# The joints between six sites of a two-part transformer kernel, worked tile by tile

## The reference

```python
def second_block(x, ...):
    for layer in range(2):
        g = norm_gains[layer]
        x = x + 0.5 * rmsnorm(swiglu(rmsnorm(x, g[0]), ...[layer, 0]), g[1])
        x = x + rmsnorm(token_mixer(rmsnorm(x, g[2]), ...), g[3])
        x = x + 0.5 * rmsnorm(swiglu(rmsnorm(x, g[4]), ...[layer, 1]), g[5])
    return x
# rmsnorm(x, g) = x * rsqrt(mean(x*x) + 1e-6) * g
# swiglu(h) = (silu(h @ w_gate) * (h @ w_up)) @ w_down,  d_ff = 2816
# token_mixer: h @ w_in, three kinds of attention (6 dilated, 4 differential,
#   6 stick-breaking heads), @ w_out
```

## Time and profile before

| what | value |
|---|---|
| three timed runs | 1581.62 us median, 1576.49 to 1591.44 |
| the profiled execution | 1580.21 us, its span 1578.4 us |
| mean granted TensorE clock in it | 0.974 |
| PE busy | 1470.2 us, 93% of the span |
| DVE, ACT, POOL busy | 958.2, 717.1, 65.0 us |
| weights and inputs moved | 246.02 MB, 156 GB/s mean |

### The profile page before, as it was taken

The page is one execution under the profiler, slowest core; times in us unless marked ns, Lnnn a source line. Parts: engine busy times, 40 slices in busy tenths (PEclk is TensorE's granted clock), DMA queues, the critical chain, the costliest instruction groups (busy, mean ns, idle before and its releaser), DMA issues.

```text
span 1578.4 us, 21810 instructions
## 1 busy us (share of the span) xinstructions
PE 1470.2 (93%) x7995; PEld 1189.5 (75%) x7995; DVE 958.2 (61%) x1503; ACT 717.1 (45%) x1215; POOL 65.0 (4%) x92
## 2 busy tenths in 40 slices
PE   5899999899996999989988999989999898799998
PEld 3778746778745888878866888868888887588886
DVE  1588235355236667775657767667676656566765
ACT  2533145222334444464575444454444555644443
POOL 0200110100101000000010000000000000100000
PEclk9999999999997999999999999989999999999999
DMA  9522264345215656644315565645656433246562
GB/s 316 181 82 79 74 214 156 107 151 152 88 61 190 210 189 200 200 150 156 108 41 186 169 224 165 201 146 176 214 169 213 147 134 108 73 141 213 167 211 74
DMA packets 187807, 246.02 MB, mean 156 GB/s; under 512 B 4224, under 2 KB 168480, under 8 KB 187488
## 3 DMA queue, kind: packets, MB, share of 16 engines
q1 hardware_dynamic: 183872, 229.43, 44.7%
q0 software_dynamic: 3296, 13.64, 2.5%
q10 hardware_dynamic: 576, 2.10, 0.4%
HBM read 244.10 MB, written 1.05 MB: 155 GB/s over the span
## 4 chain that ended last, share of the span: by engine, by line
PE 83%; DVE 6%; ACT 5%; DMA 4%; issue 2%; POOL 1%; SPq 0%; DVEq 0%; ACTq 0%; POOLq 0%
PE bank L1520 33%; PE bank L1955 20%; PE bank L1956 10%; PE bank L1609 4%; DMA weight_ring<-in_w_ada 2%; DMA weight_ring<-in_w_ffn_up 1%; PE bank L1498 1%; PE bank L1884 1%; DVE weights_low L1246 1%; ACT weights_high L835 1%; PE bank L1935 1%; PE bank L1829 1%; ACT silu_gate L869 1%; PE bank L2088 1%; PE bank L1792 1%
## 5 line engine op out<-in xcount | busy, mean ns | idle before, releaser
L1955 PE MATMUL bank<-input_split,weights_high 128*128 128x512 f32 x1408 | 503.9, 400 | 4.9 <-DVE input_split L1284 4.9
L1246 DVE TENSOR_TENSOR weights_low<-weight_ring,weights_high 128x1024 fp32r<-128x1024 f32 x328 | 396.0, 1223 | 178.3 <-ACT weights_high L835 177.4
L835 ACT ACTIVATE weights_high<-weight_ring 128x1024 fp32r<-128x1024 f32 x328 | 337.6, 1054 | 217.7 <-DMA weight_ring<-in_w_ffn_gate 70.4
L1956 PE MATMUL bank<-input_split,weights_low 128*128 128x256 f32 x1408 | 396.6, 282 | 0.0
L1955 PEld LDWEIGHTS bank<-input_split,weights_high 128*128 128x128 f32 x1408 | 266.4, 189 | 71.0 <-issue 6.0
L1956 PEld LDWEIGHTS bank<-input_split,weights_low 128*128 128x128 f32 x1408 | 267.6, 190 | 3.1
L1520 PE MATMUL bank<-weights_high,hidden_high 128*128 128x512 f32 x352 | 138.2, 393 | 1.3 <-DVE hidden_low L1326 1.3
L1520 PE MATMUL bank<-weights_low,hidden_high 128*128 128x512 f32 x352 | 137.9, 392 | 0.0
L1520 PE MATMUL bank<-weights_high,hidden_low 128*128 128x512 f32 x352 | 136.9, 389 | 0.0
L890 ACT ACTIVATE hidden_high<-hidden 128x256 fp32r<-128x256 f32 x88 | 36.8, 418 | 183.9 <-DVE hidden L1322 175.4
L1520 PE MATMUL bank<-input_split,weights_high 128*128 128x256 f32 x512 | 95.6, 288 | 0.8 <-DVE input_split L1284 0.8
(11 more groups left out here) (306 smaller groups left out, 2039.7 us busy)
## 6 DMA issues: line engine op xcount, KB each, us to landing
weight_ring<-in_w_ffn_gate SPq DMA_DIRECT2D x44, 1024.0 KB, 6.5
weight_ring<-in_w_ffn_up SPq DMA_DIRECT2D x44, 1024.0 KB, 5.8
weight_ring<-in_w_ffn_down SPq DMA_DIRECT2D x44, 1024.0 KB, 5.0
weight_ring<-in_w_in SPq DMA_DIRECT2D x42, 1024.0 KB, 5.4
weight_ring<-in_w_ada SPq DMA_DIRECT2D x24, 1024.0 KB, 6.6
weight_ring<-in_w_out SPq DMA_DIRECT2D x16, 1024.0 KB, 5.0
scaled_out<-in_norm_gains POOLq DMA_DIRECT2D x6, 512.0 KB, 4.0
gain_row<-in_norm_gains POOLq DMA_DIRECT2D x6, 512.0 KB, 3.9
```

The source lines that it names most:

```text
L835: A(unit_in(WH, U), unit_source(U), ACT.Copy).then_inc(s_high, 1)
L1246: TTn(unit_in(WL, U), unit_source(U), unit_in(WH, U).bitcast(F32), ALU.subtract).then_inc(s_low, 1)
L1955: mm(b[:, :].rearrange("p (h n) -> p h n", h=2), unit_in(WH, U)[:, k, :], HX[:, k, :, :], start=(k == 0), stop=False, skip_group_check=True)
L1956: last = mm(b[:, 0:T], unit_in(WL, U)[:, k, :], HH[:, k, :], start=False, stop=(k == KD - 1), skip_group_check=True)
```

## The change

It touches the joints and the order of the units around them.

- **Last pair of an ffn.** PE now runs `gate_up(0)`, `gate_up(1)`, `down(1)` of the pair before, and then the rows of the last two down units together, tile 0 first and tile 1 after it. `UNITS2`, the transfers and the splits follow that order; the loops are one pair shorter and that pair is written out. ACT now loads the table of the root and splits the next site's three first units ahead of `hidden_high(1)`, and DVE splits two of these ahead of `hidden_low(1)`. The mixer's `out_rows` 6 and 7 go tile by tile too.
- **Tail.** DVE does `gained`, `gained`, `update` for tile 0 and then for tile 1. ACT squares the first half of the new x of tile 0 (`x_square(i + 1, 0, 0)`) ahead of tile 1's y.
- **Norm weights.** For the first four chunks of features the scaling of x leaves the norm weights out (a tensor_scalar, no wait for the row); they are multiplied when the transposes are read from PSUM, as one number per partition, chunk by chunk. These chunks go to banks 4 and 5, two in a bank, the others to banks 2 and 3. The row fetched by POOL is half as long. PE waits for each chunk by itself.
- **Constants multiplied.** Ahead of the transposes PE multiplies the identity with 512 columns of constants into bank 0, in plain float32, four times (twelve at site 0).
- **Units in the mixer.** 30 and 31 are split after the first group's softplus (ACT) and log weights (DVE), 32 and 33 between ACT's exps of heads 3 and 4, and on DVE ahead of the log weights of the second group; 34 at the end.

```diff
+EARLY = 3
+WARM = 4
...
-                    UNITS2 += [(m, 0, "c"), (m + 1, 0, "c")] + ([(m - 1, 1, "r")] if q else []) + [(m, 1, "c"), (m + 1, 1, "c"), (m + 2, 0, "r")]
+                    back = [(m - 1, 1, "r")] if q else []
+                    late = q == FFN_PAIRS - 1
+                    UNITS2 += [(m, 0, "c"), (m + 1, 0, "c")] + ([] if late else back) + [(m, 1, "c"), (m + 1, 1, "c")] + (back if late else []) + [(m + 2, 0, "r")]
...
-                with sp.Fori(0, FFN_PAIRS - 1) as j:
+                with sp.Fori(0, FFN_PAIRS - 2) as j:
...
+                for q, src in enumerate((g, u, d)):
+                    fill(b0 + 3 * (FFN_PAIRS - 1) + q, src[FFN_PAIRS - 1], 0 if q == 2 else 256)
...
-                    load(pre_row, I["norm_gains_2"][nxt // 3, 2 * (nxt % 3)].partition_broadcast(P), "pre_loaded")
+                    load(pre_row[:, 512:D], I["norm_gains_2"][nxt // 3, 2 * (nxt % 3), 512:D].partition_broadcast(P), "pre_loaded")
...
+            def x_square(i, t, hf):
+                act.wait_ge(*(at("x_new", i - 1, t, hf) if i else at("final_scaled", t)))
+                A(unread, X[:, t, hf * 512:(hf + 1) * 512], ACT.Square, accum_out=stat[:, 2 * t + hf:2 * t + hf + 1]).then_inc(*done("sum_squares", "site", i, t, hf))
+                if hf == 0:
+                    act.wait_ge(*at("sum_squares", "site", i, t, 0))
+                    A(stat[:, 4 + t:5 + t], stat[:, 2 * t:2 * t + 1], ACT.Identity, bias=eps[:, 0:1], scale=1.0 / D).then_inc(*done("sum_squares", "site", i, t, "scaled"))
+
             def site_norm(i):
                 for t in range(2):
                     for hf in range(2):
-                        act.wait_ge(*(at("x_new", i - 1, t, hf) if i else at("final_scaled", t)))
-                        A(unread, X[:, t, hf * 512:(hf + 1) * 512], ACT.Square, accum_out=stat[:, 2 * t + hf:2 * t + hf + 1]).then_inc(*done("sum_squares", "site", i, t, hf))
-                        if hf == 0:
-                            act.wait_ge(*at("sum_squares", "site", i, t, 0))
-                            A(stat[:, 4 + t:5 + t], stat[:, 2 * t:2 * t + 1], ACT.Identity, bias=eps[:, 0:1], scale=1.0 / D).then_inc(*done("sum_squares", "site", i, t, "scaled"))
+                        if (t, hf) != (0, 0) or i == 0:
+                            x_square(i, t, hf)
                     act.wait_ge(*at("sum_squares", "site", i, t, 1))
                     A(stat[:, 8 + t:9 + t], stat[:, 2 * t + 1:2 * t + 2], ACT.Sqrt, bias=stat[:, 4 + t:5 + t], scale=1.0 / D).then_inc(*done("rms_ready", "site", i, t))
-                for b in range(4):
-                    act.wait_ge(*at("x_T", "site", i, b))
-                    A(HH[:, 2 * b:2 * b + 2, :], B[b][:, :].rearrange("p (q n) -> p q n", q=2), ACT.Copy).then_inc(*done("input_high", i, b))
+                for c in range(4):
+                    act.wait_ge(*(at("x_T", "site", i, c) if c < 2 else at("input_ready", i, c - 2)))
+                    A(HH[:, c, :], B[4 + c % 2][:, c // 2 * T:(c // 2 + 1) * T], ACT.Copy, scale=vT[:, 2, R_PRE + 8 * i + c:R_PRE + 8 * i + c + 1]).then_inc(*done("input_high", i, c))
+                for c in (4, 6):
+                    act.wait_ge(*at("x_T", "site", i, c))
+                    A(HH[:, c:c + 2, :], B[c // 2][:, :].rearrange("p (q n) -> p q n", q=2), ACT.Copy).then_inc(*done("input_high", i, c))
...
+                    if t == 0 and i < 5:
+                        x_square(i + 1, 0, 0)
...
+                a, f = last_pair, f0 + FFN_CHUNKS - 2
+                silu(0, f + 1, f - 1)
+                hidden_high(0, f + 1, a - 1)
+                high(a + 5)
+                high(a + 6)
+                silu(1, f + 2, f)
                 A(stat[:, 60:61], eps[:, 0:1], ACT.Sqrt)
+                for U in range(a + 7, min(len(UNITS2), a + 7 + EARLY)):
+                    high(U)
+                hidden_high(1, f + 2, a + 4)
...
+                    if group == SB_GROUPS[0]:
+                        high(u0 + 30)
+                        high(u0 + 31)
                 for h in range(N_SB):
+                    if h == 4:
+                        high(u0 + 32)
+                        high(u0 + 33)
                     act.wait_ge(*at("log_weight", n, h))
                     A(ZP[:, h, :], ZE[:, h, :], ACT.Exp).then_inc(*done("weight_ready", n, h))
                 A(stat[:, 60:61], eps[:, 0:1], ACT.Sqrt)
-                for U in range(u0 + 24, u0 + 29):
-                    high(U + SPLIT)
+                high(u0 + 34)
...
+                    cut = slice(0, 512)
+                    TS(XN2[:, t, cut], X[:, t, cut], stat[:, 12 + t:13 + t], None, ALU.mult).then_inc(*done("x_scaled", "site", i, t, 0))
                     dve.wait_ge(M.sem("pre_loaded"), 16 * (i + 1))
-                    for hf in range(2):
-                        cut = slice(hf * 512, (hf + 1) * 512)
-                        STT(XN2[:, t, cut], X[:, t, cut], stat[:, 12 + t:13 + t], pre_row[:, cut], ALU.mult, ALU.mult).then_inc(*done("x_scaled", "site", i, t, hf))
-                for b in range(4):
-                    dve.wait_ge(*at("input_high", i, b))
-                    TTn(HL[:, 2 * b:2 * b + 2, :], B[b][:, :].rearrange("p (q n) -> p q n", q=2), HH[:, 2 * b:2 * b + 2, :].bitcast(F32), ALU.subtract).then_inc(*done("input_ready", i, b))
+                    cut = slice(512, D)
+                    STT(XN2[:, t, cut], X[:, t, cut], stat[:, 12 + t:13 + t], pre_row[:, cut], ALU.mult, ALU.mult).then_inc(*done("x_scaled", "site", i, t, 1))
+                for c in range(4):
+                    dve.wait_ge(*at("input_high", i, c))
+                    STT(HL[:, c, :], B[4 + c % 2][:, c // 2 * T:(c // 2 + 1) * T], vT[:, 2, R_PRE + 8 * i + c:R_PRE + 8 * i + c + 1], HH[:, c, :].bitcast(F32), ALU.mult, ALU.subtract).then_inc(*done("input_ready", i, c))
+                for c in (4, 6):
+                    dve.wait_ge(*at("input_high", i, c))
+                    TTn(HL[:, c:c + 2, :], B[c // 2][:, :].rearrange("p (q n) -> p q n", q=2), HH[:, c:c + 2, :].bitcast(F32), ALU.subtract).then_inc(*done("input_ready", i, c))
...
-                gained(0, 0)
-                gained(0, 1)
-                gained(1, 0)
-                update(0)
-                gained(1, 1)
-                update(1)
+                for t in range(2):
+                    gained(t, 0)
+                    gained(t, 1)
+                    update(t)
...
+                gate_sum(0, a + 1)
+                product(0, a + 2, f + 1)
+                hidden_low(0, f + 1)
+                low(a + 5)
+                gate_sum(1, a + 3)
+                low(a + 6)
+                product(1, a + 4, f + 2)
+                ahead = range(a + 7, min(len(UNITS2), a + 7 + EARLY))
+                for U in ahead[:2]:
+                    low(U)
+                hidden_low(1, f + 2)
+                for U in ahead[2:]:
+                    low(U)
 
             def mix(i, n):
...
+                    if group == SB_GROUPS[1]:
+                        low(u0 + 32)
+                        low(u0 + 33)
                     for h in group:
 
                         dve.wait_ge(*at("z_less_sum", n, h))
                         STT(ZE[:, h, :], B[h % 4][:, 0:384], 0.0, gap, ALU.min, ALU.add).then_inc(*done("log_weight", n, h))
+                    if group == SB_GROUPS[0]:
+                        low(u0 + 30)
+                        low(u0 + 31)
                 for b in range(3):
                     dve.wait_ge(*at("attn3", n, 2 * b + 1))
                     split_out(5 + b, B[SB_OUT[b]][:, 0:T], "o_ready")
-                for U in range(u0 + 24, u0 + 29):
-                    low(U + SPLIT)
+                low(u0 + 34)
...
+                for r in hand_over(0):
+                    pe.wait_ge(*at(*r))
+                for _ in range(WARM if i else 3 * WARM):
+                    mm(B[0][:, :], ident, KB[:, 0:512], start=True, stop=True)
                 for t in range(2):
-                    for b in range(4):
-                        pe.wait_ge(*at("x_scaled", "site", i, t, b // 2))
-                        if t == 0:
-                            for r in hand_over(b, ("input_ready", i, b)):
+                    for c in (0, 2, 1, 3, 4, 5, 6, 7):
+                        pe.wait_ge(*at("x_scaled", "site", i, t, c // 4))
+                        bank, half = (4 + c % 2, c // 2) if c < 4 else (c // 2, c % 2)
+                        if t == 0 and half == 0:
+                            for r in hand_over(bank, ("input_ready", i, c + 2 if c < 4 else c)):
                                 pe.wait_ge(*at(*r))
-                        for q in range(2):
-                            c = 2 * b + q
-                            last = tr(B[b][:, q * T + t * P:q * T + (t + 1) * P], XN2[:, t, c * P:(c + 1) * P], ident)
-                        if t:
-                            last.then_inc(*done("x_T", "site", i, b))
-
```

(39 more changed lines are left out.)

63 lines of the change are left out of this document (31 added, 32 removed).

## The result

The changed kernel takes **1587.01 us** (median of 20 runs, 1581.43 to 1593.55) against 1581.10 before (20 runs, 1576.37 to 1591.44): ratio 1.0035, 95% interval 1.0019 to 1.0051. By the bound of 1% that is no change, and it lies in the predicted range. But the interval excludes 1: the change costs some 5.5 us by the ratio (5.9 by the medians), where the sum said 1.5. Executions of one kernel differ by some 12 us, and the longer ones tend to show the lower mean granted clock (here 0.988 at 1581.43 us, 0.976 at 1593.55), so a profile shows one of them.

The account below looks back on a forecast made before the run. PE, busy 93% of the span, bounds the kernel, so only its waits can give. Joints and end sites save 6.6 us, ffn ends lose 1.8, mixer ends 6.3: -1.5, profiled 1580.2 to 1581.7, median 1583, range 1571 to 1594.

Parts of the forecast that it names:

- End of a mixer: Lows of units 32 and 33 ahead of log weights 4 and 5 make PE wait: 3.15 us lost per mixer.
- End of an ffn: Root's table and three highs ahead of hidden_high(1) stall PE 0.6 us in ffn 0, 1 and 2: 1.8 lost.
- Joints: Between sites: joint 1 saves 1.7 us, joint 4 1.0, joint 3 1.5, joints 2 and 5 0.15 each.
- Site 0: First site, up to its first down: unit 3 is split 0.45 us earlier, saving 0.45.
- Last site: No square of a next x; tile 1's updates end at E + 3.3 against 4.86: 1.6 us saved.
- The clock: Joints: constants keep PE busy to E + 3.5, so transposes run at full clock, 0.11 us apart instead of 0.23.
- rival 1: Clock falls all the same, in a joint or the mixer's new wait: worst 1594, some of it 1588; chance 0.17.
- Rivals 2: New waits at mixer and ffn ends aren't there: 1575, chance 0.13; with an earlier up slot transfer 1567, chance 0.08.
- rival 3: Last down slot's transfer, issued with two more behind it, lands 5 us too late in three ffns: 1598; chance 0.06.
- The rule on transposes: Joint 2's trace disagrees with the skill's rule; by that rule the clock would be half again by the first product.

Follow-up runs that it names:

- Experiments 1 and 2: Changed kernel with units 32 and 33 split after the mixer's exps and log weights again: 1578.38 us; kernel before with the new mixer order alone: 1588.76 us.
- experiment 3: Changed kernel with hidden_high(1) and hidden_low(1) ahead of the next site's three units at the end of an ffn: 1590.45 us.
- experiment 7: Changed kernel with the first silu and hidden chunk of an ffn ahead of the split of unit 6 on ACT and DVE: 1576.51 us.
- experiment 4: Changed kernel without the matmuls of constants: 1585.36 us.
- experiment 10: Changed kernel with norm weights multiplied as a row again for all eight chunks, splits in steps of two chunks: 1586.21 us.

## Why the prediction was right, and by how much it was off

- **End of a mixer: right.** Expected 3.15 per mixer. From the first `less_sums` of heads 4 and 5 (819.90, now 824.03) to E it was 12.74 and is 15.92, 3.18 more. Experiments 1 and 2 show the cause from both sides.
- **End of an ffn: right in kind.** Expected a stall of 0.6; PE is idle 0.36 to 0.48 us, and ffn 1 and 2 are 0.8 and 0.7 longer. The reason was as given, the three `high`s. That the order also has a price if undone was not in the sum (experiment 3).
- **Joints: right step by step.** Square of y(1,0) at E + 0.78 (forecast 0.78), updates done at 4.59 (4.62), transposes from 5.25 (5.2), unit 3's slot issued at 12.31 (12.35), first down at 22.2 (22.2), with a wait of 1.7 in front of it (1 to 2). The first product came at E + 8.35 to 8.61 ("from E + 8"), and PE's own pace, put at E + 20.1 for the first down, was 20.36 once nothing held it (experiment 7). Tensor_scalar 0.49 for 0.44, a split step 0.51 for 0.45. In the mixers the second unit starts at E + 12.18 in both (11.6), so 1.2 and 0.4 us were gained where 1.7 and 1.0 were forecast.
- **Site 0: right in sign, too small.** The down came 0.9 earlier, 0.45 forecast: the up slot was issued 1.0 earlier (E + 16.54, before 17.56), and its transfer took 7.41 us against 7.52. That the two transfers were so alike is luck, as experiment 4 shows. The 3.76 us wait ahead of the down was not looked at; experiment 7 shows that all of it could be had.
- **Last site: right.** 1.6 forecast, the tail is 1.7 shorter.
- **The clock: the step that failed,** and, as far as the profiles show, most of what lies between the 1.5 of the sum and the time measured. "I take full clock" held in joints 3 and 5 only; in 1, 2 and 4 it fell (694 to 695 at 0.50, 8 transposes in 1.97), for 0.2 to 0.3 us each. The dearer falls were elsewhere: one in ffn 0 (1.7 us, as 3.4 us of half clock with PE busy) and four in the mixers, two each, where before had one in mixer 1 alone. The sum had no term for falls outside the joints. Less 3.2 for the wait and with 1.2 and 0.4 for the joints, +4.5 and +4.2 leave 2.5 and 1.4 us for them. None lay behind the new 2.65 us wait, where rival 1 looked for them, but in other kernels with that wait some did: three of fourteen. So rival 1 came half true, near its lower value (1588), at other places. One of its grounds was misread too. "A gap of 2.4 there left it full" holds for mixer 0 of the kernel before (2.41 us, ending at 805.60); in mixer 1 the same gap ended in half clock:

```profile
1346.89 1.65 PE L2088 MATMUL bank<-softplus,const_base 128*128 128x384 f32 x2 [2.42 <-POOL softplus L610]
```

```profile
1347.00:1350.00 3.00, 3.00 (x6) 1.83 (x7) 0.64 (x2) 0.00 (x0) 2.70 (x3) 0.50 0.00 0
```

- **Rivals 2 and 3 fell.** The waits are there. Of the three transfers at once rival 3 feared for the first, and it came in time; the third, the next site's up slot, is the one that came late, in ffn 1, by little here and by 1.56 us in experiment 7. The last down slot was issued at 1017.55 with two more right behind, and ACT split it at 1023.61 straight after its work before, without a wait:

```profile
1017.55 0.37 SPq L490 DMA_DIRECT2D weight_ring<-in_w_ffn_down  x1
1017.97 0.47 SPq L490 DMA_DIRECT2D weight_ring<-in_w_ffn_gate  x1
1018.48 0.58 SPq L490 DMA_DIRECT2D weight_ring<-in_w_ffn_up  x1
...
1023.28 0.42 ACT L905 ACTIVATE hidden_high<-hidden 128x256 fp32r<-128x256 f32 x1 [2.87 <-DVE hidden L1354]
1023.61 2.00 ACT L841 ACTIVATE weights_high<-weight_ring 128x1024 fp32r<-128x1024 f32 x2
```

- **The rule on transposes.** The prediction rests it on joint 2 of the kernel before, where the clock came back to full with nothing but transposes on PE. In joint 3 of the changed kernel it stays full in a window that holds nothing but transposes, and eight take 1.32 us:

```profile
1042.00:1043.00 1.00, 1.00 (x7) 0.76 (x8) 0.83 (x3) 0.63 (x3) 0.00 (x0) 1.00 0.80 328
```

The rule of the Trainium skill, TensorE: Matmul & The Clock Gate, Part 4 (PE-mode transpose), says that the full clock does not engage for them, and is not borne out by either. Nor does it explain the fall in ffn 0, which came 18 us after the last transpose. In mixer 0 three transposes stand right ahead of the 1.98 us wait, but so they do in the kernel before, where the clock stayed full.

**Open.** What makes the clock fall after 1.98 us of idleness in one kernel and not in another, with the same rows around it, isn't settled. All 14 kernels have this wait in both mixers, and in 20 of the 28 places half clock begins between 0.2 us before its end and 1.6 us after it; the kernel before is the only one that kept the full clock in both of its mixers there besides experiment 7's. The kernel of experiment 10 has its falls within 1 us of where the changed kernel has them, except one more, and its first block also ends within 0.5 us of the other's; kernels that reach the same code at other times have their falls at other places. So part of the 5.5 us may be the moment at which the code is reached and not the change; no run isolates this.

## What to carry to other kernels

An engine that works off a fixed program waits at the first instruction that isn't ready, so a part put early "because it is idle" costs what its own supplier is late, and the table of waits may name the wrong one: look for what stands behind it. Look for the wait that all gains end in (here a transfer with silu behind it) and move work out of its shadow first; only then are the other edits worth what they save. Judge the parts one by one: here one order cost 7 to 9 us and hid that all the others together gave 2 to 3. And before a difference between two profiles is put down to an edit, look at what moved in places that the edit doesn't touch: here the first block's end, one transfer and the clock moved by more than some of the parts are worth.
